# Expert blocks of 32 slots in four column groups in place of 64 slots in two, and GpSimd on two of the last additions

## The chip, the cores and the metric

One NeuronCore of a Trainium2 chip runs the whole program in one launch. The metric is the device time of one execution in microseconds (us). The kernel before took 1650.99 us, the median of 3 runs (1648.49 to 1652.93).

## What is computed

The reference is one layer of a decoder trunk for 256 prompt tokens and 64 sample tokens (320 in all), model width 1024, all in float32. First comes a mixing part (attention, retention, gMLP) and then, with which the change deals, a mixture of 32 experts of which each token uses four:

```python
logits = (x @ router_w) + router_b                 # 320 x 32
top_v, top_i = lax.top_k(logits, 4)
gates = softmax(top_v)
# for every expert e and every token that chose it
hdn = xblk @ w1[e] + b1[e]                         # 1024 -> 2048
g, up = hdn[:, :1024], hdn[:, 1024:]
g, up = minimum(g, 7), clip(up, -7, 7)
act = (up + 1) * (g * sigmoid(1.702 * g))
yb = act @ w2[e] + b2[e]                           # 1024 -> 1024
y[token] += yb * gate
x = x + g2 * y
```

The order of the additions and the size of the expert blocks are the kernel's own affair.

## The kernel before, in words

Five engines run their own programs and meet at semaphores. SyncE (SP) only issues the loads of weights, TensorE (PE) multiplies, ScalarE (ACT) and VectorE (DVE) move results out of PSUM and do the arithmetic on them, GpSimd (POOL) prepares small things and is idle in the expert part.

**Weights.** An expert has 12.6 MB of weights: four units of 2 MB for the hidden layer (units 0 to 3) and two for the layer out (units 4 and 5). They pass through `ring`, which has six slots, one for each unit number, so that the ring holds the weights of exactly one expert. SP walks over the experts; for unit j of the next expert it waits (line 366) until the last block of the expert before has used its own unit j, and then issues the load into that slot (line 367):

```python
with sp.Fori(1, NEXP) as e:
    before = sp.value_load(table_i[0:1, bass.ds(MAX_BLOCKS + 1 + e, 1)], min_val=1, max_val=MAX_BLOCKS)
    for j in range(EXPERT_UNITS):
        sp.wait_ge(unit_used, EXPERT_UNITS * before + j)
        sp.dma_start(ring[:, j, :], ins["w_moe"][bass.ds(e, 1), j, :, :].rearrange("a p n -> p (a n)")).then_inc(unit_in[j], 16)
```

`before` is the number of blocks of all experts ahead of e. PE adds one to `unit_used` each time that a block has used a unit.

**Blocks.** The tokens of an expert are put into blocks of 64 slots. A router stage on DVE counts the tokens of each expert, works out how many blocks each needs (at least one, lines 1097 to 1099), and writes a table of the expert and the first slot of each block. All four engines then loop over the blocks (`Fori(1, n_blocks + 1)`), the blocks of one expert one after another. The 64 slots are the stationary columns of the matmul, so that two matmuls, each on one half of the output columns, stand side by side in the 128 columns of the array: column group a writes partitions 64a to 64a + 63. In one block PE does, in this order:

- hidden: units 0 and 1 into one bank, 2 and 3 into a second (line 1609, 32 matmuls of 512 columns), each pair with two for the bias (line 1614)
- `scatter(i, 0)`: the block before, spread to the first 128 tokens and weighted by the gates (line 1572)
- `gather(i + 1)`: the rows of the next block's tokens, picked out by a 0/1 matrix (line 1558)
- the transposes of the activations, then those of the gates (line 1200), `scatter(i, 1)`
- layer out: unit 4 (line 1638, 8 matmuls), `turn(i + 1)`: the gathered rows of the next block transposed (line 1200), `scatter(i, 2)`, unit 5

The profile shows every float32 matmul twice, as two records; a transpose and the bfloat16 bias matmul are one each. DVE cuts the two hidden halves (lines 1167 and 1169), multiplies them (1173), adds each scattered tile to the sum `U` (1178), and picks the slots of the next block (1143, 1144, 1068, 1159). ACT does the activation (732), and copies the gathered rows (714), the transposed activations (735), the gates (738), the turned rows (718) and the output (741) out of PSUM.

**End.** After the loop DVE multiplies the sum of the three token tiles by the modulation and adds it to the residual (1182, 1184); the last block is scattered by PE into banks of its own (`FINAL_BANKS`), DVE does the same with it (1189, 1192), and SP stores the three tiles.

Of the kernel before, what the change touches and what calls it, by code (L numbers as in the profile page):

```python
# [16 lines left out]
ACT = mybir.ActivationFunctionType  # L17
AX = mybir.AxisListType
# [49 lines left out]
BLOCK = 64  # L68
MAX_BLOCKS = 64
# [58 lines left out]
def build(nc, ctx, ins, outs):  # L128
# [45 lines left out]
    def cut(at, *shape):  # L174
# [52 lines left out]
    of_block = cut(704, 2)  # L227
# [3 lines left out]
    pick_gate = cut(1024, 3, 2, BLOCK)  # L231
    sel_now = cut(1408, 2, 3)
    xgT = cut(1536, 4, 2, BLOCK)
    actT = cut(2048, 4, 2, BLOCK)
    gateT = cut(2560, 3 * P)
    y_blk = cut(2944, HALF)
    g_cut = cut(3456, HALF)
    g_act = cut(3968, HALF)
    u_cut = cut(4480, HALF)
    h_act = cut(4992, HALF)  # L240
    pick_e = cut(5504, BLOCK // 2).bitcast(BF16)

# [10 lines left out]
    xg_s = W[:, 2, 0:HALF]  # L253
# [23 lines left out]
    gate2_ready, gate2_taken, y_clean, sum_clean, qk_normed, max_ready = map(sem, (  # L277
        "gate2_ready", "gate2_taken", "y_clean", "sum_clean", "qk_normed", "max_ready"))
# [8 lines left out]
    turned, b1_in, b1_split, expert_picked = map(sem, (  # L287
        "turned", "b1_in", "b1_split", "expert_picked"))
# [28 lines left out]

    def z_banks(idx):
# [5 lines left out]
    FINAL_BANKS = [6, 0, 2]  # L324
# [57 lines left out]
    def _(pool):  # L382
# [124 lines left out]
        nc.gpsimd.memset(y_blk, 0.0).then_inc(y_clean, 1)  # L507
        pool.wait_ge(y_clean, 1)
        for a in range(2):
            pool.dma_start(y_blk[64 * a:64 * a + NEXP], ins["b2"][:, HALF * a:HALF * a + HALF]).then_inc(b2_in, 16)  # L510
        pool.wait_ge(h_ready, 3)
        nc.gpsimd.memset(U[:, :, :], 0.0).then_inc(sum_clean, 1)


    @block.scalar
    def _(act):
# [195 lines left out]
        def take_gathered(i):  # L712
            act.wait_ge(gathered, i)
            A(xg_s, ps[:, 3, :], ACT.Copy).then_inc(xg_rows, 1)  # L714

        def take_turned(i):
            act.wait_ge(turned, i)
            A(xgT, ps[:, 3, :].rearrange("p (c a s) -> p c a s", c=4, a=2), ACT.Copy).then_inc(xg_ready, 1)
# [8 lines left out]
        act.wait_ge(b2_in, 32)  # L727
        act.sem_inc(y_ready, 1)
        n_blocks = act.value_load(table_i[0:1, MAX_BLOCKS:MAX_BLOCKS + 1], min_val=NEXP, max_val=MAX_BLOCKS - 1)
        with act.Fori(1, n_blocks + 1) as i:  # L730
            act.wait_ge(g_cut_ready, i)
            A(g_act, g_cut, ACT.Gelu_apprx_sigmoid).then_inc(g_act_ready, 1)  # L732
            take_gathered(i + 1)
            act.wait_ge(actT_done, i)
            A(actT, ps[:, 4, :].rearrange("p (c a s) -> p c a s", c=4, a=2), ACT.Copy).then_inc(actT_ready, 1)
            act.wait_ge(gateT_done, i)
            act.wait_ge(scattered, 3 * i)
            A(gateT[:, 0:TOKENS], ps[:, 5, 0:TOKENS], ACT.Copy).then_inc(gateT_ready, 1)  # L738
# [6 lines left out]
    def _(dve):  # L745
# [320 lines left out]
        def pick_slots():  # L1066

            X.tensor_tensor(pick, iota.unsqueeze(1).to_broadcast([P, 3, BLOCK]), sel_now[:, 0, :].unsqueeze(2).to_broadcast([P, 3, BLOCK]), ALU.is_equal).then_inc(picked, 1)  # L1068

# [4 lines left out]
        done(X.memset(gateT, 0.0), added)  # L1074
# [20 lines left out]
        X.tensor_copy(counted, aux_bank("cnt")[:, 0:NEXP]).then_inc(used("cnt"), 1)  # L1095
        aux_taken(dve, "cnt")
        done(X.tensor_scalar(n_of, counted, float(BLOCK), 1.0, ALU.is_gt, ALU.add))
        for m in range(2, TOKENS // BLOCK):
            done(X.scalar_tensor_tensor(out=n_of, in0=counted, scalar=float(BLOCK * m), in1=n_of, op0=ALU.is_gt, op1=ALU.add))
# [36 lines left out]
        done(X.tensor_copy(pick_gate[:, :, :, 0:NEXP], gate_e.unsqueeze(2).to_broadcast([P, 3, 2, NEXP])), gates_ready)  # L1136
# [43 lines left out]
        dve.wait_ge(added, 3 * n_blocks + 1)  # L1180
        for t, r in enumerate(ROWS):
            X.tensor_tensor(U[0:r, t, :], U[0:r, t, :], V[0:r, 2 if t == 2 else 0, :], ALU.mult).then_inc(scaled, 1)
            dve.wait_ge(scaled, t + 1)
            X.tensor_tensor(R[0:r, t, :], R[0:r, t, :], U[0:r, t, :], ALU.add).then_inc(summed, 1)
            dve.wait_ge(summed, t + 1)
        for t, r in enumerate(ROWS):
            dve.wait_ge(scattered, 3 * n_blocks + t + 1)
            first = FINAL_BANKS[t]
            X.tensor_tensor(U[0:r, t, :].rearrange("p (a b) -> p a b", a=2), ps[0:r, first:first + 2, :],
                            V[0:r, 2 if t == 2 else 0, :].rearrange("p (a b) -> p a b", a=2), ALU.mult).then_inc(scaled, 1)  # L1190
            dve.wait_ge(scaled, 3 + t + 1)
# [4 lines left out]
    def _(pe):  # L1196
# [356 lines left out]
        def gather(n):  # L1553

            pe.wait_ge(picked, n)
            for t, r in enumerate(ROWS):
                for a in range(2):
                    last = mm(ps[64 * a:64 * a + 64, 3, :], pick[0:r, t, :], T[0:r, t, HALF * a:HALF * a + HALF],  # L1558
                              start=(t == 0), stop=(t == 2), skip_group_check=True)
            last.then_inc(gathered, 1)  # L1560

        def turn(n):

            pe.wait_ge(xg_rows, n)
            for c in range(4):
                last = tr(ps[:, 3, c * P:(c + 1) * P], xg_s[:, c * P:(c + 1) * P], P)
            last.then_inc(turned, 1)

        def scatter_tile(t, first):

            for a in range(2):
                last = mm(ps[:, first + a, :], gateT[64 * a:64 * a + 64, t * P:(t + 1) * P], y_blk[64 * a:64 * a + 64, :], start=True, stop=True)  # L1572
            last.then_inc(scattered, 1)

        def scatter(n, t):

            pe.wait_ge(added, 3 * n + t - 2)
            scatter_tile(t, 6)

        def filled(j):  # L1580

# [180 lines left out]
```

## Time and profile before

| what | value |
|---|---|
| median of 3 runs | 1650.99 us (1648.49 to 1652.93) |
| the profiled execution, its own time | 1649.28 us |
| its span, first to last instruction | 1647.5 us |
| mean granted TensorE clock | 0.965 of full speed |
| PE busy / its weight loads busy | 1548.8 us (94%) / 661.6 us (40%) |
| DVE / ACT / POOL busy | 474.2 / 318.8 / 108.9 us |
| moved by DMA | 491.95 MB, mean 299 GB/s |

A busy PE is one that has a matmul in flight. The span is what the views of the trace divide; the time of the execution is 1.8 us longer. The expert loop runs from 648.9 us to the end, 60% of the span, and everything that the change touches lies in it, in the few microseconds of routing ahead of it, or behind it.

### The profile page before, as it was taken

The page shows a single profiled execution, that of the slowest core. Times are in us where ns is not written, and L with a number is a line of the kernel's source. Part 1 is how long each engine was busy: PE and PEld are TensorE (multiplying, and loading weights), DVE is VectorE, ACT ScalarE, POOL GpSimd, SP SyncE. Part 2 cuts the span into 40 slices and gives each one's busy share as a digit, 9 for nine tenths or more (in the row PEclk, how much of TensorE's full clock was granted, in tenths as well). Part 3 has the DMA queues.
Part 4 walks back from the last instruction along what each step waited for, and adds up shares of the span by engine and source line. Part 5 has one row for each costly group of instructions (what it writes and reads, how often), then busy time and mean ns, then how long its engine had stood idle before and what let it go on. Part 6 is the DMA issues. An engine that isn't in the chain of part 4 may idle for free.

```text
span 1647.5 us, 20298 instructions
## 1 busy us (share of the span) xinstructions
PE 1548.8 (94%) x8093; PEld 661.6 (40%) x8094; DVE 474.2 (29%) x791; ACT 318.8 (19%) x579; POOL 108.9 (7%) x111
## 2 busy tenths in 40 slices
PE   4989899978989898999999999999999999999996
PEld 4555555545544455333333333333333333333332
DVE  2141222147346254222222222222222222222224
ACT  1123332120231232111111111111111111111110
POOL 0000000120433250000000000000000000000000
PEclk8989998898998997999999999999999999999999
DMA  9462441341332650999999999999593999999993
GB/s 355 185 257 111 194 164 58 115 145 64 128 126 105 240 193 32 415 425 429 428 429 428 428 429 429 428 429 428 239 408 161 415 427 429 429 427 429 429 427 130
DMA packets 38583, 491.95 MB, mean 299 GB/s; under 512 B 4784, under 2 KB 4912, under 8 KB 9744
## 3 DMA queue, kind: packets, MB, share of 16 engines
q1 hardware_dynamic: 34144, 477.33, 70.1%
q0 software_dynamic: 4400, 14.06, 2.8%
q8 instruction: 29, 0.48, 0.1%
q14 instruction: 10, 0.08, 0.0%
HBM read 487.05 MB, written 4.33 MB: 298 GB/s over the span
## 4 chain that ended last, share of the span: by engine, by line
PE 89%; DVE 4%; DMA 3%; ACT 2%; issue 1%; POOL 1%; SPq 0%; DVEq 0%; POOLq 0%; ACTq 0%
PE ps L1609 28%; PE ps L1264 17%; PE ps L1638 15%; PE ps L1572 6%; PE ps L1558 6%; PE ps L1271 4%; PE ps L1200 4%; DMA ring<-in_w_dense 2%; PE ps L1223 1%; PE ps L1216 1%; PE ps L1614 1%; PE ps L1322 1%; PE ps L1342 1%; ACT ring L555 1%; PE ps L1520 1%
## 5 line engine op out<-in xcount | busy, mean ns | idle before, releaser
L1609 PE MATMUL ps<-ring,arena 128*64 128x512 f32 x2176 | 480.2, 594 | 2.9 <-issue 2.9
L1264 PE MATMUL ps<-ring,xT 128*128 128x512 f32 x672 | 306.2, 613 | 3.2 <-DMA ring<-in_w_dense 2.4
L1609 PEld LDWEIGHTS ps<-ring,arena 128*64 128x64 f32 x2176 | 156.7, 137 | 308.2 <-issue 305.6
L1638 PE MATMUL ps<-ring,arena 128*64 128x512 f32 x1088 | 248.5, 598 | 0.0
L1178 DVE TENSOR_TENSOR U<-ps,U 128x1024 f32<-128x1024 f32 (+1 forms) x102 | 124.4, 1220 | 248.9 <-PE ps L1572 248.9
L1264 PEld LDWEIGHTS ps<-ring,xT 128*128 128x128 f32 x672 | 129.2, 196 | 162.6 <-issue 158.2
L1638 PEld LDWEIGHTS ps<-ring,arena 128*64 128x64 f32 x1088 | 72.1, 136 | 168.1 <-issue 142.3
L1572 PE MATMUL ps<-arena 64*128 64x512 f32 x420 | 119.7, 636 | 0.8 <-ACT arena L741 0.8
L1558 PE MATMUL ps<-T,arena 128*64 128x512 f32 (+1 forms) x420 | 104.3, 615 | 1.2 <-DVE arena L1068 1.2
L714 ACT ACTIVATE W<-ps 128x512 f32<-128x512 f32 x35 | 20.9, 598 | 338.5 <-PE ps L1558 338.5
L1169 DVE TENSOR_SCALAR arena<-ps 128x512 f32<-128x512 f32 x34 | 23.5, 692 | 217.5 <-PE ps L1614 217.5
L1271 PE MATMUL ps<-ring,xT 128*64 128x256 f32 x672 | 81.6, 398 | 0.0
L1167 DVE TENSOR_SCALAR arena<-ps 128x512 f32<-128x512 f32 x34 | 23.5, 692 | 187.6 <-PE ps L1614 187.6
L1271 PEld LDWEIGHTS ps<-ring,xT 128*64 128x64 f32 x672 | 48.4, 143 | 33.0 <-issue 12.7
L732 ACT ACTIVATE arena<-arena 128x512 f32<-128x512 f32 x34 | 21.4, 629 | 204.6 <-DVE arena L1167 204.6
L555 ACT ACTIVATE ring<-ps 128x512 f32<-128x512 f32 (+1 forms) x48 | 23.4, 487 | 170.0 <-PE ps L1264 141.4
L1558 PEld LDWEIGHTS ps<-T,arena 128*64 128x64 f32 (+1 forms) x420 | 24.1, 136 | 76.5 <-issue 76.5
L738 ACT ACTIVATE arena<-ps 128x320 f32<-128x320 f32 x34 | 14.9, 437 | 203.5 <-PE ps L1572 203.5
L1200 PEld LDWEIGHTS ps<-consts,arena 128*128 128x128 f32 (+2 forms) x321 | 35.2, 138 | 41.5 <-issue 41.1
L1200 PE MATMUL ps<-consts,arena 128*128 128x128 f32 (+2 forms) x321 | 48.2, 277 | 0.5 <-ACT arena L629 0.5
L1216 PE MATMUL ps<-ring 128*32 128x128 f32 x768 | 29.2, 317 | 18.8 <-DMA ring<-in_w_dense 18.8
L1572 PEld LDWEIGHTS ps<-arena 64*128 64x128 f32 x420 | 33.7, 190 | 29.6 <-issue 29.6
(261 smaller groups left out, 1043.7 us busy)
## 6 DMA issues: line engine op xcount, KB each, us to landing
ring<-in_w_moe SPq DMA_DIRECT2D x192, 2048.0 KB, 14.5
ring<-in_w_dense SPq DMA_DIRECT2D x33, 2048.0 KB, 8.6
V<-in_state POOLq DMA_DIRECT2D x6, 256.0 KB, 8.2
out_sample_retention<-V POOLq DMA_DIRECT2D x6, 256.0 KB, 2.8
R<-in_x_prompt SPq DMA_DIRECT2D x1, 1024.0 KB, 17.1
arena<-in_cache_kT POOLq DMA_DIRECT2D x8, 128.0 KB, 3.5
arena<-in_cache_v POOLq DMA_DIRECT2D x8, 128.0 KB, 3.6
arena<-in_b_gate POOLq DMA_DIRECT2D x4, 256.0 KB, 4.4
```

The lines of the kernel that those rows point to most:

```text
L555: A(buf[0:ROWS[t], t, c0 + c:c0 + c + w], src, func).then_inc(z_used, 1)
L1167: X.tensor_scalar(g_cut, ps[:, 0, :], LIMIT, None, ALU.min).then_inc(g_cut_ready, 1)
L1169: X.tensor_scalar(u_cut, ps[:, 1, :], LIMIT, -LIMIT, ALU.min, ALU.max).then_inc(dve_step, 1)
L1178: X.tensor_tensor(both, ps[0:r, 6:8, :], both, ALU.add).then_inc(added, 1)
L1200: return nc.tensor.transpose(out, in_, ident[0:r, 0:r], **kw)
L1216: last = mm(aux_bank(name)[32 * j:32 * j + 32, 0:128], silu_c[:, k, :], wv[:, k, 128 * j:128 * j + 128], start=(k == 0), stop=(k == KD - 1 ...
L1264: last = mm(banks[t][0], xT[:, k, t * P:t * P + P], wv[:, k, :], start=(k == 0), stop=(k == KD - 1))
L1271: last = mm(banks[2 + a][0], xT[:, k, 2 * P:TOKENS], wv[:, k, 256 * a:256 * a + 256], start=(k == 0), stop=(k == KD - 1), skip_group_check ...
L1558: last = mm(ps[64 * a:64 * a + 64, 3, :], pick[0:r, t, :], T[0:r, t, HALF * a:HALF * a + HALF], start=(t == 0), stop=(t == 2), skip_group_ ...
L1572: last = mm(ps[:, first + a, :], gateT[64 * a:64 * a + 64, t * P:(t + 1) * P], y_blk[64 * a:64 * a + 64, :], start=True, stop=True)
L1609: last = mm(ps[64 * a:64 * a + 64, half, :], xgT[:, k, j % 2, :], wv[:, k, HALF * a:HALF * a + HALF], start=(j % 2 == 0 and k == 0), stop= ...
L1638: last = mm(ps[64 * a:64 * a + 64, 2, :], actT[:, k, j - 4, :], wv[:, k, HALF * a:HALF * a + HALF], start=(j == 4 and k == 0), stop=(j == ...
```

## The change

A block has 32 slots in place of 64, and up to 72 blocks are allowed for. The 32 slots are the stationary columns of a matmul, and four column groups of 32, each on a quarter of the output columns, stand side by side. A unit of the hidden layer now holds two of the eight slices of the contraction, with all 2048 output columns, so that all four hidden units add to one bank; the weights are laid out on the host to fit. Gather, scatter and the layer out work in quarters of 256 columns, and a scatter uses four row groups of 32 slots in place of two of 64. Tiles 0 and 1 of a scatter go together ahead of the gather, tile 2 stays between unit 4 and unit 5; the transposes of the gates move to the end of the block. Ring, slots, SP's loop and its waits are the same. At the end POOL multiplies and adds the sums of tiles 0 and 1 (two operations each), DVE that of tile 2.

```diff
-BLOCK = 64
-MAX_BLOCKS = 64
+BLOCK = 32
+MAX_BLOCKS = 72
+QUARTER = 256
+GROUPS = D // QUARTER
...
+        pool.wait_ge(table_ready, 1)
+        n_blocks = pool.value_load(table_i[0:1, MAX_BLOCKS:MAX_BLOCKS + 1], min_val=NEXP, max_val=MAX_BLOCKS - 1)
+        for t in range(2):
+            pool.wait_ge(added, 3 * n_blocks + t + 1)
+            nc.gpsimd.tensor_tensor(U[:, t, :], U[:, t, :], V[:, 0, :], ALU.mult).then_inc(pool_scaled, 1)
+            pool.wait_ge(pool_scaled, t + 1)
+            nc.gpsimd.tensor_tensor(R[:, t, :], R[:, t, :], U[:, t, :], ALU.add).then_inc(pool_summed, 1)
...
             act.wait_ge(g_cut_ready, i)
             A(g_act, g_cut, ACT.Gelu_apprx_sigmoid).then_inc(g_act_ready, 1)
+            act.wait_ge(actT_done, i)
+            A(actT, ps[:, OUT, 0:QUARTER].rearrange("p (c a s) -> p c a s", c=2, a=GROUPS), ACT.Copy).then_inc(actT_ready, 1)
             take_gathered(i + 1)
...
             take_turned(i + 1)
+            act.wait_ge(scattered, 2 * i)
             act.wait_ge(unit_used, EXPERT_UNITS * i + 5)
-            A(y_blk, ps[:, 2, :], ACT.Copy).then_inc(y_ready, 1)
+            A(y_blk, ps[:, OUT, 0:QUARTER], ACT.Copy).then_inc(y_ready, 1)
+            act.wait_ge(gateT_done, i + 1)
+            A(gateT[:, 0:TOKENS], ps[:, GATES, 0:TOKENS], ACT.Copy).then_inc(gateT_ready, 1)
...
             for t, r in enumerate(ROWS):
-                dve.wait_ge(scattered, 3 * i + t - 2)
-                both = U[0:r, t, :].rearrange("p (a b) -> p a b", a=2)
-                X.tensor_tensor(both, ps[0:r, 6:8, :], both, ALU.add).then_inc(added, 1)
+                dve.wait_ge(scattered, 2 * i - 1 if t < 2 else 2 * i)
+                by_group = U[0:r, t, :].rearrange("p (a c) -> p a c", a=GROUPS)
+                at = QUARTER * (t % 2)
+                X.tensor_tensor(by_group, ps[0:r, SCAT:SCAT + GROUPS, at:at + QUARTER], by_group, ALU.add).then_inc(added, 1)
...
-            for half in range(2):
-                for j in (2 * half, 2 * half + 1):
-                    pe.wait_ge(unit_in[j], 16 * e + 16 * (filled(j) + 1))
-                    wv = ring[:, j, :].rearrange("p (k c) -> p k c", k=4)
-                    for k in range(4):
-                        for a in range(2):
-                            last = mm(ps[64 * a:64 * a + 64, half, :], xgT[:, k, j % 2, :], wv[:, k, HALF * a:HALF * a + HALF],
-                                      start=(j % 2 == 0 and k == 0), stop=False, skip_group_check=True)
...
+            for j in range(4):
+                pe.wait_ge(unit_in[j], 16 * e + 16 * (filled(j) + 1))
+                wv = ring[:, j, :].rearrange("p (k a c) -> p k a c", k=2, a=GROUPS)
+                for k in range(2):
+                    c, b = divmod(2 * j + k, GROUPS)
+                    for a in range(GROUPS):
+                        last = mm(ps[32 * a:32 * a + 32, HID, :], xgT[:, c, b, :], wv[:, k, a, :],
+                                  start=(j == 0 and k == 0), stop=False, skip_group_check=True)
...
             pe.wait_ge(y_ready, i)
             pe.wait_ge(gateT_ready, i)
-            scatter(i, 0)
-            gather(i + 1)
+            scatter_prompt(3 * i)
+            pe.wait_ge(picked, i + 1)
+            gather(0)
+            gather(1)
             pe.wait_ge(act_ready, i)
-            for c in range(4):
-                last = tr(ps[:, 4, c * P:(c + 1) * P], h_act[:, c * P:(c + 1) * P], P)
+            for c in range(2):
+                last = tr(ps[:, OUT, c * P:(c + 1) * P], h_act[:, c * P:(c + 1) * P], P)
             last.then_inc(actT_done, 1)
...
-            scatter(i, 1)
+            gather(2).then_inc(gathered, 1)
...
                 if j == 4:
                     turn(i + 1)
-                    scatter(i, 2)
+                    pe.wait_ge(added, 3 * i + 2)
+                    scatter_tile(2, SCAT, 0).then_inc(scattered, 1)
+            pe.wait_ge(gates_picked, i)
+            for t, r in enumerate(ROWS):
+                last = tr(ps[:, GATES, t * P:t * P + r], pick_gate[0:r, t, :, :], r)
+            last.then_inc(gateT_done, 1)
```

PE, from the wait for unit 5 to the first unit of the next block. In these rows `x7` counts matmuls (not records) of one kind, sizes are output rows x columns, and the semaphores are those that the first one waits for; `ring` holds the weights, `arena` the small operands. Before, the end of the loop and its beginning:

```order
L1638 MATMUL ps<-ring,arena 64x512 [waits unit_in5]
L1638 MATMUL ps<-ring,arena 64x512 x7
L1598 ISA
L1598 COMPARE_AND_BRANCH
...
L1605 ISA [waits expert_picked,xg_ready]
L1609 MATMUL ps<-ring,arena 64x512 [waits unit_in0]
L1609 MATMUL ps<-ring,arena 64x512 x7
L1609 MATMUL ps<-ring,arena 64x512 [waits unit_in1]
```

and now:

```order
L1656 MATMUL ps<-ring,arena 32x256 [waits unit_in5]
L1656 MATMUL ps<-ring,arena 32x256 x15
L1219 MATMUL ps<-consts,arena 128x128 [waits gates_picked]
L1219 MATMUL ps<-consts,arena 128x128
L1219 MATMUL ps<-consts,arena 128x64
L1618 ISA
L1618 COMPARE_AND_BRANCH
...
L1624 ISA [waits expert_picked,xg_ready]
L1629 MATMUL ps<-ring,arena 32x512 [waits unit_in0]
L1629 MATMUL ps<-ring,arena 32x512 x7
```

Between unit 5 of a block and unit 0 of the next stand now the three transposes of the gates, and a unit out is 16 matmuls of 256 columns where it was 8 of 512.

PE, between the last hidden matmul and unit 4, now (before, there were one scatter tile, six gather matmuls, four transposes of the activations, three of the gates and a second scatter tile at this place):

```order
L1634 MATMUL ps<-consts,arena 32x512 x4
L1596 REGISTER_ALU [waits gateT_ready,y_ready]
L1591 MATMUL ps<-arena 128x256 [waits added]
L1591 MATMUL ps<-arena 128x256 x7
L1641 REGISTER_ALU
L1576 MATMUL ps<-T,arena 32x256 [waits picked]
L1576 MATMUL ps<-T,arena 32x256 x7
L1219 MATMUL ps<-consts,arena 128x128 [waits act_ready]
L1219 MATMUL ps<-consts,arena 128x128
L1576 MATMUL ps<-T,arena 32x256 x4
L1656 MATMUL ps<-ring,arena 32x256 [waits unit_in4,actT_ready]
```

The third tile of the gather now stands between the transposes of the activations and unit 4, and both scatters of prompt tokens stand ahead of the gather.

## Rows read from the trace of the kernel before

**Rows 1.** Page: span; busy time, share and instructions of each engine.
```profile
span 1647.5 us, 20298 instructions
PE 1548.8 (94%) x8093; PEld 661.6 (40%) x8094; DVE 474.2 (29%) x791; ACT 318.8 (19%) x579; POOL 108.9 (7%) x111
```
**Rows 2.** Lines 1167 and 1609: count, ns min/median/max, first and last start in us, shape.
```profile
L1167 DVE TENSOR_SCALAR arena<-ps x34: 691/692/692, 657.9 to 1609.9; 128x512 f32<-128x512 f32 x34
...
L1609 PE MATMUL ps<-ring,arena x2176: 590/592/1061, 648.9 to 1616.1; 128*64 128x512 f32 x198
```
**Rows 3.** Stretches: us, busy PE, PEld, DVE, ACT, POOL (count), granted clock, DMA share, GB/s.
```profile
700.00:1140.00 440.00, 440.00 (x2061) 147.29 (x2059) 105.75 (x167) 70.04 (x107) 0.00 (x0) 1.00 1.01 428
...
1156.00:1173.66 17.66, 17.66 (x83) 5.96 (x83) 5.62 (x10) 3.98 (x6) 0.00 (x0) 1.00 0.07 28
1173.66:1181.30 7.64, 7.64 (x40) 2.60 (x38) 0.69 (x1) 0.63 (x1) 0.00 (x0) 1.00 0.88 332
```
**Rows 4.** Expert weights: issues, KB each, median us to landing; then line 367's min/median/max.
```profile
ring<-in_w_moe SPq DMA_DIRECT2D x192, 2048.0 KB, 14.5
...
DMA to landing us min/median/max: 7.5/14.5/23.0
```
**Rows 5.** Timeline of PE, one block: start, us, line, records.
```profile
1148.11 7.04 PE L1609 MATMUL ps<-ring,arena 128*64 128x512 f32 x32
1154.98 0.39 PE L1614 MATMUL ps<-consts,arena 96*64 96x512 bf16 x2
1155.30 1.13 PE L1572 MATMUL ps<-arena 64*128 64x512 f32 x4
1156.36 2.94 PE L1558 MATMUL ps<-T,arena 128*64 128x512 f32 x12
1159.23 1.08 PE L1200 MATMUL ps<-consts,arena 128*128 128x128 f32 x7
1160.05 1.18 PE L1572 MATMUL ps<-arena 64*128 64x512 f32 x4
1161.16 3.65 PE L1638 MATMUL ps<-ring,arena 128*64 128x512 f32 x16
...
1166.39 3.65 PE L1638 MATMUL ps<-ring,arena 128*64 128x512 f32 x16
1169.87 7.04 PE L1609 MATMUL ps<-ring,arena 128*64 128x512 f32 x32
```
**Rows 6.** Timeline of PE, the first matmuls with four column groups of 32.
```profile
19.27 3.64 PE L1216 MATMUL ps<-ring 128*32 128x128 f32 x64 [4.36 <-DMA ring<-in_w_dense]
...
36.37 1.96 PE L1216 MATMUL ps<-ring 128*32 128x128 f32 x64 [2.95 <-DMA ring<-in_w_dense]
```
**Rows 7.** Stretches, as rows 3: those two, and the start of the expert loop.
```profile
19.20:22.90 3.70, 3.63 (x64) 2.96 (x64) 0.00 (x0) 0.00 (x0) 0.00 (x0) 0.50 1.03 269
...
36.30:38.30 2.00, 1.93 (x64) 1.69 (x64) 0.19 (x1) 0.00 (x0) 0.87 (x2) 1.00 0.96 399
...
648.80:654.40 5.60, 5.51 (x18) 1.82 (x20) 0.00 (x0) 0.08 (x1) 0.00 (x0) 0.70 0.01 3
```
**Rows 8.** Timeline, start of the expert loop.
```profile
648.89 8.78 PE L1609 MATMUL ps<-ring,arena 128*64 128x512 f32 x32 [2.90 <-issue]
654.42 11.06 SPq L367 DMA_DIRECT2D ring<-in_w_moe  x4
```
**Rows 9.** Groups by line (page): busy us, mean ns of one, idle before, releaser.
```profile
L1178 DVE TENSOR_TENSOR U<-ps,U 128x1024 f32<-128x1024 f32 (+1 forms) x102 | 124.4, 1220 | 248.9 <-PE ps L1572 248.9
...
L738 ACT ACTIVATE arena<-ps 128x320 f32<-128x320 f32 x34 | 14.9, 437 | 203.5 <-PE ps L1572 203.5
```
**Rows 10.** The end: timeline of DVE and SP; one line of POOL.
```profile
1642.89 1.22 DVE L1192 TENSOR_TENSOR R<-R,U 64x1024 f32<-64x1024 f32 x1
1644.13 0.53 SPq L372 DMA_DIRECT2D out_y_sample<-R  x1
...
L476 POOL TENSOR_TENSOR ring<-ring x3: 2333/2337/3322, 518.5 to 523.1; 128x1024 f32<-128x1024 f32 x2, 64x1024 f32<-64x1024 f32 x1
```

More of the change, by code:

```diff
@@ L1094, in _ @@
         counted = rtmp[:, 1, :]
[L1095 removed]
+        X.tensor_scalar(counted, aux_bank("cnt")[:, 0:NEXP], 1.0 / BLOCK, None, ALU.mult).then_inc(used("cnt"), 1)
         aux_taken(dve, "cnt")
[L1097 to L1099 removed]
+        limits = TOKENS // BLOCK - 1
+        done(X.tensor_tensor(over, counted.unsqueeze(2).to_broadcast([P, NEXP, limits]),
+                             iota[:, 1:1 + limits].unsqueeze(1).to_broadcast([P, NEXP, limits]), ALU.is_gt))
+        done(X.tensor_reduce(n_of, over, AX.X, ALU.add))
+        done(X.tensor_scalar(n_of, n_of, 1.0, None, ALU.add))
         done(X.tensor_tensor_scan(out=cum_of, data0=ones[:, 0:NEXP], data1=n_of, initial=0.0, op0=ALU.mult, op1=ALU.add))
@@ L1551, in _, with gather, scatter_tile, scatter_prompt @@
            start=True, stop=True).then_inc(aux_ready, 1)
[L1553 to L1560, printed above, removed]
+        def gather(t):
+            r = ROWS[t]
+            for a in range(GROUPS):
+                last = mm(ps[32 * a:32 * a + 32, ROWSB, 0:QUARTER], pick[0:r, t, :], T[0:r, t, QUARTER * a:QUARTER * a + QUARTER],
+                          start=(t == 0), stop=(t == 2), skip_group_check=True)
+            return last
         def turn(n):
             pe.wait_ge(xg_rows, n)
-            for c in range(4):
-                last = tr(ps[:, 3, c * P:(c + 1) * P], xg_s[:, c * P:(c + 1) * P], P)
+            for c in range(2):
+                last = tr(ps[:, ROWSB, c * P:(c + 1) * P], xg_s[:, c * P:(c + 1) * P], P)
             last.then_inc(turned, 1)
[L1569 to L1580, printed above, removed]
-            return DENSE_UNITS // DENSE_SLOTS if j < DENSE_SLOTS else 0
+        def scatter_tile(t, first, at):
+            r = ROWS[t]
+            for a in range(GROUPS):
+                last = mm(ps[0:r, first + a, at:at + QUARTER], gateT[32 * a:32 * a + 32, t * P:t * P + r], y_blk[32 * a:32 * a + 32, :], start=True, stop=True)
+            return last
+        def scatter_prompt(waited):
+            pe.wait_ge(added, waited)
+            scatter_tile(0, SCAT, 0)
+            scatter_tile(1, SCAT, QUARTER).then_inc(scattered, 1)
         pe.wait_ge(gate2_taken, 4)
-        gather(1)
+        pe.wait_ge(picked, 1)
+        for t in range(3):
+            last = gather(t)
+        last.then_inc(gathered, 1)
         turn(1)
@@ L1595, in _ @@
         pe.wait_ge(b1_split, 12)
+        pe.sem_inc(gateT_done, 1)
         pe.sem_inc(unit_used, EXPERT_UNITS - 1)
@@ L1618, in _ @@
+            for a in range(GROUPS):
+                last = mm(ps[32 * a:32 * a + 32, HID, :], pick_e[0:96], b1_by_group[0:96, :, a, :],
+                          start=False, stop=True, skip_group_check=True)
+            last.then_inc(unit_used, 1)
             pe.wait_ge(y_ready, i)
             pe.wait_ge(gateT_ready, i)
-            scatter(i, 0)
-            gather(i + 1)
+            scatter_prompt(3 * i)
+            pe.wait_ge(picked, i + 1)
+            gather(0)
+            gather(1)
@@ L1634, in _ @@
                 pe.wait_ge(unit_in[j], 16 * e + 16 * (filled(j) + 1))
-                wv = ring[:, j, :].rearrange("p (k c) -> p k c", k=4)
-                for k in range(4):
-                    for a in range(2):
-                        last = mm(ps[64 * a:64 * a + 64, 2, :], actT[:, k, j - 4, :], wv[:, k, HALF * a:HALF * a + HALF],
-                                  start=(j == 4 and k == 0), stop=(j == 5 and k == 3), skip_group_check=True)
+                wv = ring[:, j, :].rearrange("p (k c) -> p k c", k=GROUPS)
+                for b in range(GROUPS):
+                    for a in range(GROUPS):
+                        last = mm(ps[32 * a:32 * a + 32, OUT, 0:QUARTER], actT[:, j - 4, b, :], wv[:, b, QUARTER * a:QUARTER * a + QUARTER],
+                                  start=(j == 4 and b == 0), stop=(j == 5 and b == 3), skip_group_check=True)
                 last.then_inc(unit_used, 1)
```

118 lines of the change are left out of this document (54 added, 64 removed).

## The prediction

> **What bounds the kernel now.** I read the page first, then the expert loop block by block, then the loads. The page shows PE busy for 94% of the span [rows 1]. Line 1167 runs once per block: 34 times, its starts 952.0 us apart from first to last [rows 2], so that a block takes 952.0 / 33 = 28.85 us, and all blocks the same. In the stretch from 700 to 1140 us PE is busy throughout at the full clock, and so is DMA, at 428 GB/s [rows 3]. The two nearly tie: six units of 2048 KB are 12.58 MB, 29.4 us of loads per expert against 28.85 us of PE. Who waits for whom shows where an expert has two blocks: PE works on without a gap, while DMA falls to 28 GB/s for 17.66 us [rows 3], since the ring holds one expert and a slot comes free only in the expert's last block. So PE sets the pace, and DMA has almost nothing to spare: 31 experts x 6 units x 4.89 us (2.097 MB at 429 GB/s) = 909.5 us of pure loading lie within a loop of 998.6.
>
> **How many blocks.** Counting the choices of the reference's router on its inputs, 8 experts have at most 32 tokens, 22 have 33 to 64, and two have 66. With 64 slots that gives 30 + 2 x 2 = 34 blocks, as the trace has it [rows 2]; with 32 slots 8 + 44 + 6 = 58. The last expert and the first have one block each.
>
> **The change on PE.** A record of 512 columns takes 6.87 / 32 = 0.215 us in the stream of pairs [rows 5], with two side by side. Four column groups are to be seen in line 1216: 64 records of 128 columns in 1.96 us, 31 ns each with the run-out of the last [rows 6]; one by itself would take 2 x 0.215 x 128 / 512 = 0.107 us, so 3.5 of four at least ran at once, and without the run-out all four. I take 0.107 us per record of 512 and 0.054 per record of 256. A new unit is 16 records of 512 or 32 of 256: 1.72 us either way, where it was 3.44. A transpose is 0.107 us, and turning from one kind of matmul to another costs 0.1 to 0.3 us (12 gather records from 1156.36 to 1159.23: 2.87 us for 2.58 of work [rows 5]); I take 0.2. One block is then four hidden units 6.88, bias 0.42, two scatter tiles 1.06, two gather tiles 1.06, two transposes 0.41, gather 0.63, unit 4 1.92, turn 0.41, scatter 0.63, unit 5 1.92, gates 0.52: **15.9 us**. 58 such blocks are 922 us where 34 x 28.85 were 981. The page "TensorE: Matmul & The Clock Gate" of the Trainium skill (Part 3, "Measured speedup vs the span model") gives three column groups as 2.38 times one; by that ratio hidden and unit out would be a quarter longer, and the sum below some 30 us higher; the trace's 1.96 us speaks against it.
>
> No row has four row groups (the scatter). Two at once have a row: 4 records of 512 in 1.06 us [rows 5]. A tile costs 0.43 us if all four run at once, 0.86 in pairs; I take 0.43, and the other adds 0.9 us ahead of unit 4, where, below, 1.5 us are free.
>
> **The change on the loads.** This is the term that decides. Loads, slots and waits are the same; when a slot comes free is not. In a two-block expert the first block needs all six units and frees none. Once unit 5 has landed, nothing is left to load until the second block has used unit 0. Behind that landing PE does unit 5 (1.92), the transposes of the gates (0.52), which stand there now, and unit 0 of the second block (1.72 and the run-out of its last record, 0.592 - 0.215 = 0.38 [rows 2]): 4.5 us. Then the load starts from nothing: the fastest landing of a unit is 7.5 us [rows 4] for 4.89 of transfer, so 2.6 us are lost to the start. The trace has such a restart: unit 0 of a second block is done at 1169.87 + 3.44 + 0.38 = 1173.69 [rows 5], and from there the rate comes back [rows 3]. **Each of the 24 experts with two or three blocks thus stops the loads for 4.5 + 2.6 = 7.1 us**, a three-block one for another whole block, 15.9. Such an expert takes 29.4 + 7.1 = 36.5 us, for two blocks of 15.9: PE waits, and the loads with their stops set the pace. One-block experts run at 29.4.
>
> Before, these stops hit two experts and cost nothing beyond PE's own 28.85; now they hit 24.
>
> **The sum, on the span.**
> - First slot free: was 654.4, after 16 records from 648.89 on, much of them at half clock [rows 7, 8]. At half clock 16 new ones take 3.4 and the run-out 0.4: 652.7.
> - Loading 186 units: 909.5.
> - 25 starts from nothing (the first and 24) x 2.6: 65.
> - 24 x 4.5 us of PE between last landing and first free slot: 108.
> - Two whole middle blocks: 31.8.
> - Behind the last landing: unit 5 2.1, the copies of output and gates by ACT (0.44 for 320 columns [rows 9]) 1.1, scatter 1.3, six DVE operations of 1.22 and a gap = 7.5, and the store, 3.4 from the last DVE operation to the end of the span [rows 1, 10]: 15.4.
>
> Together 1782.4. POOL's four operations take 2.33 us each [rows 10] and start with the last block's first addition, some 5 us ahead of the last landing; they end ahead of DVE's turn and cost nothing, and if they did not, some 3 us.
>
> DVE has three additions of 1.22 per block [rows 9], in all about 7 us of work in a block of 16 to 18; ACT has less. Both lie under PE's work and waits, at no cost; uncovered, an addition held up would push the scatter behind unit 4, where 1.5 us are free (PE is through with that scatter 8.3 us after unit 3 landed, unit 5 lands after 9.8). The routing ahead of the loop has a compare and a reduction over 288 numbers in place of three small operations, under half a us.
>
> **The clock.** PE now waits up to 4.9 - 1.7 = 3.2 us for units 2 and 3. A wait of 2.95 us left the granted clock at 1.00 (64 records in 1.96 us, 2.4 GHz), one of 4.36 us did not (3.64 us, 0.50, 1.2 GHz) [rows 6, 7]. Bounds: nothing, or 4.3 us of work from unit 3 to unit 4 at half clock in each of the 24, less the 1.5 free: 2.8 x 24 = 67. Being nearer to 2.95, I take a third, 22.
>
> 1782.4 + 22.3 = 1804.7 for the span. The profiled execution took 1649.28 for a span of 1647.5; with the same 1.8 the forecast is **1806 us**, 157 over that execution (the median of the runs shown is 1.7 higher still).
>
> **Rivals.**
> - *The clock is lost in every such expert* and is still low in the stop: 67 in place of 22, and 3.8 us of unit 5, transposes and unit 0 twice as long, x 24 = 91: 1782.4 + 158 + 1.8 = **1942**. For it: 4.36 us was enough, and short bursts may not bring the clock back: it was 0.50 in the burst behind that wait [rows 7]. Against: PE works almost without a gap from unit 3 to unit 5. The Trainium skill's "TensorE: Matmul & The Clock Gate" ("HAM oscillation") describes this very case, a matmul that waits for each slice of its weights and runs each at the lower clock; by it this rival would be the likeliest, and the 2.95 us row disagrees.
> - *The other side: the loads do not stop.* If a slot came free before the last unit of its expert had landed, only loading would remain: 652.7 + 2.6 + 909.5 + 15.4 + 1.8 = **1582**. The point that decides is the stop's length: below (1649 - 1582) / 24 = 2.8 us the change would gain. For it: PE's work does shrink from 981 to 922 us. Against: the start alone costs 2.6, and the one stop shown lasted as long as PE needed [rows 3].
> - *The groups don't run four at a time* but two, so that the change doesn't do what it says: hidden 13.8, out 6.9, the rest as before, about 28 us x 58 = 1640, from 648.9 on: **2310**. Against: line 1216 [rows 6].
>
> **Chances.** Forecast 0.73 (its own range 1770 to 1850), clock rival, whole or half, 0.18, loads without a stop 0.04, pairs 0.03, anything else 0.02. The low end of the range is the sum without the clock term and with turns of 0.1 us, 1770; the high end takes in about half of the clock rival, 1880. A measurement here tells 0.3%, 5 us, from no change: slower 0.95, same 0.01, faster 0.04.
>
> **What would show it.** In the profile after: 58 records where line 1167 had 34; hidden units of 1.7 us with waits for DMA ahead of them; PE busy well below 90% of the loop; in each two-block expert a stretch of about 5 us with DMA near 0 GB/s between the last landing and the next issue; a period near 36.5 us for such experts and 29.4 for the others; a few granted clocks of 0.50. Wrong would be a loop without such gaps, a period of 32 us or less for two-block experts, or hidden units of 3.4 us at the full clock.

## The result and the profile after

The changed kernel takes **1790.97 us** (median of 3 runs, 1786.05 to 1797.63), 1.085 times the kernel before [95% interval 1.081 to 1.090]. The forecast was 1806, with a range of 1770 to 1880. The profiled execution took 1797.63 us for a span of 1795.8, the longest of the three.

The page of the changed kernel: span; busy time, share and instructions; the chain that ended last by engine; and the costliest group (busy us, mean ns | idle before it, and what ended that).

```profile
span 1795.8 us, 34114 instructions
PE 1535.4 (86%) x14371; PEld 697.0 (39%) x14372; DVE 578.6 (32%) x1050; ACT 374.7 (21%) x747; POOL 121.0 (7%) x116
...
PE 55%; DMA 38%; DVE 3%; ACT 2%; issue 1%; POOL 1%; SPq 0%; DVEq 0%; POOLq 0%; ACTq 0%
...
L1629 PE MATMUL ps<-ring,arena 128*32 128x512 f32 x3712 | 468.8, 647 | 143.9 <-DMA ring<-in_w_moe 140.9
```

PE is busy 13 us less than before [rows 1], but the span is 148 us longer. Ahead of the hidden matmuls (line 1629, line 1609 before) it now waits 141 us for loads, and 38% of the last chain is DMA. The once-per-block instruction, the first cut on DVE, shows that the blocks are as many as counted, where [rows 2] had 34:

```profile
L1185 DVE TENSOR_SCALAR arena<-ps x58: 424/424/426, 658.8 to 1772.5; 128x256 f32<-128x256 f32 x58
```

Here is PE's timeline from the first block of a two-block expert to its second (start, us, line, records, wait in brackets).

```profile
1128.81 1.92 PE L1629 MATMUL ps<-ring,arena 128*32 128x512 f32 x16 [0.49 <-DMA ring<-in_w_moe]
1133.70 2.77 PE L1629 MATMUL ps<-ring,arena 128*32 128x512 f32 x16 [2.97 <-DMA ring<-in_w_moe]
...
1140.42 1.93 PE L1656 MATMUL ps<-ring,arena 128*32 128x256 f32 x32
1142.28 0.44 PE L1219 MATMUL ps<-consts,arena 128*128 128x128 f32 x2
1142.65 0.66 PE L1591 MATMUL ps<-arena 32*64 32x256 f32 x8
1143.48 1.93 PE L1656 MATMUL ps<-ring,arena 128*32 128x256 f32 x32 [0.17 <-DMA ring<-in_w_moe]
1145.35 0.64 PE L1219 MATMUL ps<-consts,arena 128*128 128x128 f32 x3
1145.92 7.07 PE L1629 MATMUL ps<-ring,arena 128*32 128x512 f32 x64
1152.81 0.40 PE L1634 MATMUL ps<-consts,arena 96*32 96x512 bf16 x4
1153.14 1.15 PE L1591 MATMUL ps<-arena 32*128 32x256 f32 x16
1154.22 1.07 PE L1576 MATMUL ps<-T,arena 128*32 128x256 f32 x16
```

Unit 5 lands at 1143.44. From there PE does unit 5, the three transposes of the gates, and, from 1145.92, unit 0 of the second block. SP issues the next load at 1148.05, 4.6 us after the landing. The table of stretches (us, busy PE, PEld, DVE, ACT, POOL, granted clock, DMA share, GB/s) shows that nothing moves in that time, and what follows:

```profile
1143.45:1147.95 4.50, 4.47 (x55) 1.95 (x59) 2.26 (x5) 2.10 (x3) 0.00 (x0) 1.00 0.00 0
1147.95:1155.62 7.67, 7.67 (x90) 2.79 (x84) 2.23 (x5) 0.42 (x1) 0.00 (x0) 1.00 0.89 333
1155.62:1180.10 24.48, 19.33 (x238) 7.46 (x237) 8.39 (x14) 4.82 (x10) 0.00 (x0) 1.00 0.96 410
```

The stretches of 0 and of 333 GB/s are the stop and the start from nothing; in [rows 3], before, the loads ran at 428 GB/s and stopped only in the two experts with two blocks. From the landing times of unit 5, one expert to the next: 29.37 us in the six experts with one block, 36.6 to 36.9 in nineteen with two, 37.1 to 37.9 in three more of them, 52.2 and 52.4 in the two with three blocks.

### The profile page after: what moved, and what is told of

Read it like the earlier page. It is cut to its first block, busy times and chain, and to the rows that moved or that the text cites. A ratio compares the mean times of both kernels' runs of the same rounds, so it can differ in the third digit from the quotient of the medians.

```text
span 1795.8 us, 34114 instructions
## 1 busy us (share of the span) xinstructions
PE 1535.4 (86%) x14371; PEld 697.0 (39%) x14372; DVE 578.6 (32%) x1050; ACT 374.7 (21%) x747; POOL 121.0 (7%) x116
## 4 chain that ended last, share of the span: by engine, by line
PE 55%; DMA 38%; DVE 3%; ACT 2%; issue 1%; POOL 1%; SPq 0%; DVEq 0%; POOLq 0%; ACTq 0%
DMA ring<-in_w_moe 35%; PE ps L1283 15%; PE ps L1629 12%; PE ps L1656 8%; PE ps L1290 4%; PE ps L1219 3%; PE ps L1591 3%; PE ps L1576 3%; DMA ring<-in_w_dense 2%; PE ps L1242 1%; PE ps L1235 1%; PE ps L1341 1%; PE ps L1361 1%; ACT ring L570 1%; PE ps L1539 0%
## 5 line engine op out<-in xcount | busy, mean ns | idle before, releaser
L1629 PE MATMUL ps<-ring,arena 128*32 128x512 f32 x3712 | 468.8, 647 | 143.9 <-DMA ring<-in_w_moe 140.9
L1629 PEld LDWEIGHTS ps<-ring,arena 128*32 128x32 f32 x3712 | 112.0, 114 | 436.9 <-issue 221.0
L1196 DVE TENSOR_TENSOR U<-ps,U 128x1024 f32<-128x1024 f32 x174 | 206.9, 1217 | 132.7 <-PE ps L1591 132.6
L1656 PE MATMUL ps<-ring,arena 128*32 128x256 f32 x3712 | 224.3, 382 | 21.9 <-DMA ring<-in_w_moe 21.6
L1656 PEld LDWEIGHTS ps<-ring,arena 128*32 128x32 f32 x3712 | 108.7, 109 | 129.8 <-DMA ring<-in_w_moe 35.0
L1591 PE MATMUL ps<-arena 32*128 32x256 f32 (+1 forms) x1416 | 113.1, 421 | 0.7 <-issue 0.7
L1576 PE MATMUL ps<-T,arena 128*32 128x256 f32 (+1 forms) x1416 | 101.9, 390 | 0.8 <-DVE arena L1083 0.8
L1219 PE MATMUL ps<-consts,arena 128*128 128x128 f32 (+2 forms) x491 | 100.2, 292 | 1.0 <-ACT arena L729 0.5
L1591 PEld LDWEIGHTS ps<-arena 32*128 32x128 f32 (+1 forms) x1416 | 59.2, 180 | 60.6 <-issue 58.1
L747 ACT ACT_TABLE_LOAD x58 | 74.4, 1283 | 2.1 <-issue 1.1
L1177 DVE TENSOR_TENSOR arena<-arena 128x384 f32<-128x384 f32 x58 | 32.4, 558 | 97.7 <-PE ps L1219 95.8
L1576 PEld LDWEIGHTS ps<-T,arena 128*32 128x32 f32 (+1 forms) x1416 | 34.0, 108 | 42.2 <-issue 32.2
```

Source lines behind the costliest of these rows:

```text
L1196: X.tensor_tensor(by_group, ps[0:r, SCAT:SCAT + GROUPS, at:at + QUARTER], by_group, ALU.add).then_inc(added, 1)
L1219: return nc.tensor.transpose(out, in_, ident[0:r, 0:r], **kw)
L1576: last = mm(ps[32 * a:32 * a + 32, ROWSB, 0:QUARTER], pick[0:r, t, :], T[0:r, t, QUARTER * a:QUARTER * a + QUARTER], start=(t == 0), stop= ...
L1591: last = mm(ps[0:r, first + a, at:at + QUARTER], gateT[32 * a:32 * a + 32, t * P:t * P + r], y_blk[32 * a:32 * a + 32, :], start=True, sto ...
L1629: last = mm(ps[32 * a:32 * a + 32, HID, :], xgT[:, c, b, :], wv[:, k, a, :], start=(j == 0 and k == 0), stop=False, skip_group_check=True)
L1656: last = mm(ps[32 * a:32 * a + 32, OUT, 0:QUARTER], actT[:, j - 4, b, :], wv[:, b, QUARTER * a:QUARTER * a + QUARTER], start=(j == 4 and b ...
```

## Experiments

Beside the median stands the **loading time** of the profiled execution, because the part ahead of the expert loop ended some 10 us sooner or later from one execution to the next. It runs from the landing of the last unit of the first expert that SP's loop loads to the last landing of all. It is 1092.04 us in the changed kernel (686.62 to 1778.66) and 927.76 in the one before. It can differ by 2.6 us between two executions of the same loop: experiment 5, which leaves the loop as it is, has 1089.48. The kernel before was run beside all of them: 1649.6 us (11 runs) and 1648.2 (17 runs).

The theory is that of the prediction: loads with their stops set the pace. The rivals are a price per block, wherever it lies, and the lost clock.

### 1. One block for every expert

```diff
-        done(X.tensor_scalar(n_of, n_of, 1.0, None, ALU.add))
+        done(X.tensor_scalar(n_of, n_of, 0.0, 1.0, ALU.mult, ALU.add))
```

> The changed kernel with one block per expert: tokens beyond an expert's first 32 are left out, so 32 blocks in place of 58, and no expert has a second block. Stopped loads (each of 24 experts holds all six slots until its second block uses unit 0): only pure loading is left, 686.6 us (landing of the first loaded expert) + 30 x 29.37 + 17.1 behind the last landing + 1.8 = 1587 us, DMA at 428 GB/s without a gap. Price per block (the 58 blocks themselves, at (1791 - 649) / 58 = 19.7 us each, are what became longer): 32 blocks would be worth 630 us, and the loads a floor of 910, so also about 1587; but then DMA would already lie near its ceiling in the changed kernel. Lost clock: PE waits most of the time here and the clock falls most often, so if the clock set the pace this would stay above 1650.

Measured: 1584.36 us (2 runs), 0.960 of the kernel before [0.956, 0.965]. Every expert takes 29.33 to 29.38 us. In the long stretch the loads never stop (columns as above), though the granted clock is at 0.86:

```profile
700.00:1560.00 860.00, 570.52 (x5451) 183.97 (x5443) 170.65 (x319) 106.64 (x203) 0.00 (x0) 0.86 1.01 428
```

So without second blocks only loading remains, and PE's half clock, 265 us of the expert loop in this execution, costs nothing where PE waits anyway.

### 2. The gates' transposes out of the stop

```diff
                     scatter_tile(2, SCAT, 0).then_inc(scattered, 1)
-            pe.wait_ge(gates_picked, i)
-            for t, r in enumerate(ROWS):
-                last = tr(ps[:, GATES, t * P:t * P + r], pick_gate[0:r, t, :, :], r)
-            last.then_inc(gateT_done, 1)
+                    pe.wait_ge(gates_picked, i)
+                    for t, r in enumerate(ROWS):
+                        last = tr(ps[:, GATES, t * P:t * P + r], pick_gate[0:r, t, :, :], r)
+                    last.then_inc(gateT_done, 1)
```

They now stand between units 4 and 5, ahead of the last landing.

> The three transposes of the gates moved from behind unit 5 to ahead of the wait for unit 5. PE does the same work in all. Stopped loads: 0.5 us less between last landing and first free slot, in each of 24 experts, so 12 us less (1791 to 1779), and 36.25 us in place of 36.75 per two-block expert. PE's total work or the clock: no change within 5 us.

Measured: 1781.6 us (6 runs), 1.080 of before [1.077, 1.084], 9.4 less than the change as it is; the loading time is 1079.62, 12.4 less. PE's timeline around a stop, from the landing of unit 5 at 1134.18 to the next issue at 1138.54:

```profile
1134.05 0.64 PE L1219 MATMUL ps<-consts,arena 128*128 128x128 f32 x3
1134.62 1.93 PE L1656 MATMUL ps<-ring,arena 128*32 128x256 f32 x32
1136.42 7.07 PE L1629 MATMUL ps<-ring,arena 128*32 128x512 f32 x64
```

The same work, moved by one place, gains because it leaves the stop. That is no price per block: the work is still done 58 times. The gain splits: where unit 5 was not late the stop fell from 4.61 to 3.97 us, the full length of the transposes; where the clock had been low before it, as here, only to some 4.3, since the transposes use up the slack ahead of unit 5 and delay it. That makes 9 of the 12.4 us; 2 more are three late starts of unit 5 in the changed kernel's execution (below), which not every execution has.

### 3. The gates' transposes five times

```diff
-            for t, r in enumerate(ROWS):
-                last = tr(ps[:, GATES, t * P:t * P + r], pick_gate[0:r, t, :, :], r)
+            for _ in range(5):
+                for t, r in enumerate(ROWS):
+                    last = tr(ps[:, GATES, t * P:t * P + r], pick_gate[0:r, t, :, :], r)
```

> The three transposes of the gates done five times behind unit 5, 12 more of them, some 1.3 us per block at the full clock. Stopped loads: 24 stops longer by 1.3 and the two three-block experts' middle blocks too: 26 x 1.3 = 34 us more (1825). Price per block: 58 x 1.3 = 75 us more (1866). One-block experts keep 29.4 us by the first and lengthen by the second.

Measured: 1862.56 us (4 runs), 1.128 of before [1.123, 1.132]: 72 more, by the number alone the rival's result. The form is the theory's: one-block experts still take 29.36 us, two-block ones 38.9 to 39.2 or 40.5 to 40.8. PE's timeline at two of the stops:

```profile
1043.00 3.39 PE L1656 MATMUL ps<-ring,arena 128*32 128x256 f32 x32 [1.81 <-DMA ring<-in_w_moe]
1046.32 3.12 PE L1219 MATMUL ps<-consts,arena 128*128 128x128 f32 x15
1049.37 7.07 PE L1629 MATMUL ps<-ring,arena 128*32 128x512 f32 x64
...
1062.42 1.93 PE L1656 MATMUL ps<-ring,arena 128*32 128x256 f32 x32
1064.28 2.93 PE L1219 MATMUL ps<-consts,arena 128*128 128x128 f32 x15
1067.14 3.21 PE L1629 MATMUL ps<-ring,arena 128*32 128x512 f32 x28
```

The first stop is a first block's, with the clock low in unit 5 (3.32 us from start to start); the second stretch is a second block, at full clock. Fifteen transposes take 2.86 us (1064.28 to 1067.14), 0.19 each, so that 2.29 were added and not the 1.3 that I had expected with 0.107 each. And in 12 of the 24 stops the clock was low, 1.6 us more. 24 x 2.29 + 12 x 1.6 + 2 middle blocks x 2.28 = 79, less the 2 that late starts of unit 5 cost in the changed kernel (below): 77. The loading time grew by 76.1. The theory stands, my price of a transpose fell.

### 4. PE kept busy ahead of unit 3

```diff
             for j in range(4):
+                if j == 3:
+                    pe.wait_ge(added, 3 * i)
+                    for _ in range(8):
+                        mm(ps[0:32, SCAT, 0:128], ident[:, 0:32], ident, start=True, stop=True)
                 pe.wait_ge(unit_in[j], 16 * e + 16 * (filled(j) + 1))
```

The spare matmuls fill part of the 2.97 us wait and write where nobody reads.

> Before the wait for unit 3 PE does eight small matmuls into a bank that the scatter overwrites later (16 records, 1.7 us), so that it does not sit idle there; nothing is left out. It measures what the lost clock costs in the changed kernel. Clock worth little (it is lost in gaps whose delay the next wait absorbs): the granted clock rises above 0.94 and the time stays at 1791 within 5 us (the two three-block experts' middle blocks add 3.4, a few us come back). Clock worth the 22 us of the prediction or more: 1770 or less.

Measured: 1809.49 us (6 runs), 1.097 of before [1.093, 1.101]: 18.5 more, which neither side had. The clock now held through unit 3 in every such expert. But in 9 of 24 it was lost one wait later, ahead of unit 5, as PE's timeline shows for two experts next to each other:

```profile
1035.42 1.93 PE L1660 MATMUL ps<-ring,arena 128*32 128x256 f32 x32 [1.80 <-DMA ring<-in_w_moe]
1037.29 0.64 PE L1219 MATMUL ps<-consts,arena 128*128 128x128 f32 x3
1037.86 5.36 PE L1633 MATMUL ps<-ring,arena 128*32 128x512 f32 x48
...
1062.26 1.92 PE L1633 MATMUL ps<-ring,arena 128*32 128x512 f32 x16
...
1072.05 3.62 PE L1660 MATMUL ps<-ring,arena 128*32 128x256 f32 x32 [1.81 <-DMA ring<-in_w_moe]
1075.60 0.64 PE L1219 MATMUL ps<-consts,arena 128*128 128x128 f32 x3
1076.17 4.07 PE L1633 MATMUL ps<-ring,arena 128*32 128x512 f32 x36
```

Unit 3 of the second, at 1062.26, runs at the full clock. The same wait ahead of unit 5, and that unit takes 1.87 us in one expert and 3.55 in the other. There the loss lies in the stop, which is 4.61 us in fifteen experts and 6.1 to 6.3 in the nine. 9 x 1.6, and 1.72 of spare matmuls in each of the two middle blocks, less the 2: 15.8, and the loading time grew by 15.8. So a lost clock costs where it falls into the stop, and next to nothing ahead of it.

### 5. The end without GpSimd

```diff
-            nc.gpsimd.tensor_tensor(U[:, t, :], U[:, t, :], V[:, 0, :], ALU.mult).then_inc(pool_scaled, 1)
...
+            X.tensor_tensor(U[:, t, :], U[:, t, :], V[:, 0, :], ALU.mult).then_inc(pool_scaled, 1)
```

and so with the addition behind it: DVE does both for tiles 0 and 1.

> The changed kernel without GpSimd's part: DVE does the multiplications and additions of tiles 0 and 1 itself behind the loop. Read on the stretch from the last landing of a weight unit to the end of the span, 17.1 us in the changed kernel. If sharing with GpSimd helps: DVE has four more operations of 1.25 us behind its last addition, the stretch grows to about 20 us. If it does not, because GpSimd and DVE slow each other down there (DVE's addition on tile 2 took 3.25 us beside GpSimd, where it takes 1.22 alone): 17 us or less. Either way under 0.2% of the time.

Measured, in one run: 1793.79 us. The last landing is at 1772.7, the end of the span at 1792.0: 19.3 us, against 17.1 with GpSimd (1778.66 to 1795.8). The sharing is worth 2.1 us, in one execution of each (with the clock lost in the last expert in both), not the 4 x 1.23 that DVE no longer does. Why, the timelines of the end show: DVE, then POOL, of the changed kernel, and DVE's same two operations in this experiment.

```profile
1779.86 1.22 DVE L1199 TENSOR_TENSOR U<-U,V 64x1024 f32<-64x1024 f32 x1
1781.11 3.25 DVE L1201 TENSOR_TENSOR R<-R,U 64x1024 f32<-64x1024 f32 x1
1784.57 1.23 DVE L1208 TENSOR_TENSOR U<-ps,V 128x1024 f32<-128x1024 f32 x1 [0.20 <-DVE R L1201]
1785.83 1.83 DVE L1211 TENSOR_TENSOR R<-R,U 128x1024 f32<-128x1024 f32 x1
```

```profile
1775.17 2.37 POOL L525 TENSOR_TENSOR U<-U,V 128x1024 f32<-128x1024 f32 x1 [1147.10 <-DVE U L1196]
1777.62 2.37 POOL L527 TENSOR_TENSOR R<-R,U 128x1024 f32<-128x1024 f32 x1
1779.95 3.34 POOL L525 TENSOR_TENSOR U<-U,V 128x1024 f32<-128x1024 f32 x1
1783.37 3.21 POOL L527 TENSOR_TENSOR R<-R,U 128x1024 f32<-128x1024 f32 x1
```

```profile
1778.70 1.21 DVE L1196 TENSOR_TENSOR U<-U,V 64x1024 f32<-64x1024 f32 x1
1779.94 1.22 DVE L1198 TENSOR_TENSOR R<-R,U 64x1024 f32<-64x1024 f32 x1
```

The addition to `R` takes DVE 3.25 us beside POOL and 1.22 without it.

### 6. The next block's units 0 and 1 ahead of the layer out

The slots of units 0 and 1 now come free before units 4 and 5 are even used; units 4 and 5 count in a semaphore of their own, and the gather and turn of the next block move up.

```diff
-                sp.wait_ge(unit_used, EXPERT_UNITS * before + j)
+                if j < 4:
+                    sp.wait_ge(unit_used, 4 * before + j)
+                else:
+                    sp.wait_ge(out_used, 2 * before + (j - 4))
...
+            turn(i + 1)
+            e_next = pe.value_load(table_i[0:1, bass.ds(i, 1)], min_val=0, max_val=NEXP - 1)
+            pe.wait_ge(xg_ready, i + 1)
+            hidden(0, e_next)
+            hidden(1, e_next)
 
             pe.wait_ge(actT_ready, i)
```

> Hidden units 0 and 1 of the next block moved ahead of the layer out of the current one (turn and third gather tile moved ahead with them), so that a second block frees slots 0 and 1 before units 4 and 5 of its expert have landed; SP waits for units 0 to 3 and for 4 and 5 on two counters. PE's work is the same. Stopped loads: the stop of 7 us disappears in 22 two-block experts and shrinks to about 14 us in the two three-block ones; the pace becomes PE's 31 us in runs of two-block experts and DMA's 29.4 elsewhere: 1640 to 1670 us. Price per block or clock: no change, 1780 to 1800.

Measured: 1682.86 us (4 runs), 1.019 of before [1.014, 1.024]; the loading time is 982.39, 110 less. A two-block expert takes 30.9 to 31.2 us behind a one-block expert, and 32.3 to 32.9 in a row of such experts. The stops shrink to 0.6 us at most, save 16.9 and 16.6 in the two experts with three blocks, and with them go three quarters of the loss (108 of 141 us, by the medians). The time missed the expected 1640 to 1670, because PE becomes the bound. Its timeline in one block of 16.3 us (970.60 to 986.92):

```profile
969.04 1.01 PE L1222 MATMUL ps<-consts,arena 128*128 128x128 f32 x4
970.60 3.64 PE L1630 MATMUL ps<-ring,arena 128*32 128x512 f32 x32 [0.55 <-ACT arena L736]
974.05 1.92 PE L1671 MATMUL ps<-ring,arena 128*32 128x256 f32 x32
...
986.92 3.64 PE L1630 MATMUL ps<-ring,arena 128*32 128x512 f32 x32 [0.55 <-ACT arena L736]
```

PE waits 0.55 us for ACT's copy of the turned rows, which the new order put on its path.

### 7. As 6, with the gates' transposes in that gap and the third scatter tile behind unit 5

Against experiment 6:

```diff
             turn(i + 1)
+            pe.wait_ge(gates_picked, i)
+            for t, r in enumerate(ROWS):
+                last = tr(ps[:, GATES, t * P:t * P + r], pick_gate[0:r, t, :, :], r)
+            last.then_inc(gateT_done, 1)
             e_next = pe.value_load(table_i[0:1, bass.ds(i, 1)], min_val=0, max_val=NEXP - 1)
...
-                if j == 4:
-                    pe.wait_ge(added, 3 * i + 2)
-                    scatter_tile(2, SCAT, 0).then_inc(scattered, 1)
...
+            pe.wait_ge(added, 3 * i + 2)
+            scatter_tile(2, SCAT, 0).then_inc(scattered, 1)
```

> As the run with the next block's hidden units 0 and 1 ahead of the layer out, with like matmuls put together: the gates' transposes stand beside the turn, where PE waited 0.55 us per block, and the third scatter tile behind unit 5. With the stops gone PE's own block sets the pace in runs of two-block experts (16.3 us there). If that is the bound now: two changes of the array's division fewer and the wait filled, about 15.5 us per block, 31 per two-block expert, and 1683 falls to 1645 to 1655, even with the kernel before. If something else is (a remaining stop of the loads): no change from 1683.

Measured: 1656.11 us (12 runs), 1.006 of before [1.003, 1.009]. PE's timeline of one whole block, 959.99 to 975.60:

```profile
959.99 3.64 PE L1630 MATMUL ps<-ring,arena 128*32 128x512 f32 x32
...
966.43 1.43 PE L1222 MATMUL ps<-consts,arena 128*128 128x128 f32 x7
967.99 3.64 PE L1630 MATMUL ps<-ring,arena 128*32 128x512 f32 x32
971.44 3.64 PE L1675 MATMUL ps<-ring,arena 128*32 128x256 f32 x64
975.01 0.66 PE L1594 MATMUL ps<-arena 32*64 32x256 f32 x8
975.60 3.64 PE L1630 MATMUL ps<-ring,arena 128*32 128x512 f32 x32
```

A block of 15.6 us makes a two-block expert 31.2, above the 29.4 of loading and the 28.85 of one 64-slot block [rows 2]. This is the best order of 32-slot blocks that I found. It ends 0.6% behind the kernel before; no version here that computes every token beats that one.

## Why the prediction was right, point by point

- **First slot free**: forecast 652.7, measured 653.45.
- **PE's work**: right in kind. Sixteen hidden records take 1.72 us, four column groups run at once, and so do the scatter's four row groups, which no row before had shown: 16 records of 256 columns in 1.08 us (1153.14 to 1154.22), in fours that start within 0.02 us, the fours 0.22 us apart once they run. Line 1283, without groups, needs 0.43 us per record of 512, so that each four took the time of one. The Trainium skill's "TensorE: Matmul & The Clock Gate" (Part 3, "Measured speedup vs the span model") gives four row groups as 3.07 times one. The trace doesn't agree: those fours ran as four. A middle block took 15.5 us where the sum had 15.9; a transpose alone was mispriced (0.19 us, not 0.107 and a turn).
- **The stop**: forecast 4.5 us, measured 4.61 in 21 of the 24. Experiments 1, 2 and 6 show that it is the cause: without second blocks no stop and no loss, half a us of work out of it shortens it by up to its length, and slots freed early take 110 of the loss away.
- **The start from nothing**: forecast 2.6 us, measured 36.75 - 29.36 - 4.61 = 2.8. That and the stop's 0.1, over the 24 experts, are 7 of the sum's miss.
- **The clock**: the term that failed, 22 us forecast ("I take a third") and 2.2 measured in the loop. The clock was lost more often than that: PE needs 3.15 us from the start of unit 3 to the gather at full clock, 4.5 to 4.8 in fourteen of the 24 experts and 5.3 to 6.0 in three. The Trainium skill's "TensorE: Matmul & The Clock Gate" ("HAM oscillation") has this mechanism, and by it the clock rival would have been the likeliest; the trace agrees that the clock falls, not that it costs. What was mis-sized was the price, 2.8 us each. Most losses are 1.4 to 1.7 us, and the slack ahead of unit 5 is 1.8 (the wait of experiment 4), not 1.5. Only three overran it, by 1.0, 1.0 and 0.3, and how many do varies from run to run: in experiment 5, with the same loop, the clock was lost in 13 of the 24, none overran, and all stops are 4.61, but for the two that a middle block lengthens. One of the three, with unit 5 starting at 753.78 for a landing at 752.78:

```profile
743.03 3.64 PE L1629 MATMUL ps<-ring,arena 128*32 128x512 f32 x16 [1.76 <-DMA ring<-in_w_moe]
...
749.02 1.07 PE L1576 MATMUL ps<-T,arena 128*32 128x256 f32 x16
...
753.78 1.93 PE L1656 MATMUL ps<-ring,arena 128*32 128x256 f32 x32
```

- **The end**: forecast 15.4 us, measured 17.1. The step was "they end ahead of DVE's turn and cost nothing, and if they did not, some 3 us": POOL ended at 1786.58, between DVE's last operations, and DVE lost 2.0 us in one addition and 0.6 in another. The step alone is not the whole 1.7: in experiments 1 and 4 the additions took the same 3.27 and 1.83 us, and the end 15.7. There the clock held in the last expert, and DVE came to tile 2 some 1.7 us ahead of the last landing; in the changed kernel's execution it was lost (unit 3 to the gather 4.8 us), DVE came only with the landing, and the held-up addition was in the way of the last block. So 1.4 of the 1.7 needed the lost clock too.
- **The sum** without the clock term was 1782.4 for a span of 1795.8: 0.8 from the first slot, 1.2 from the first loaded expert (33.2 us, 31.9 forecast), 9.5 from the two-block experts (the 7, and 2.2 of the clock), 1.7 from the end. With 22 for the clock it came out 9 above that span, and the forecast 15 above the median. That it is so near is in part luck: an excess in one term covered small deficits in four.

The rival on the other side, loads without a stop, gave 1582 as the time; experiment 1, which makes its condition true by leaving out all tokens past an expert's first 32, took 1584.

## What to carry to other kernels

When a buffer holds exactly one set of operands, look for the place where the last load has landed and the first slot is not yet free: everything between these two points is paid in full, once per set that is used twice, and making the work elsewhere faster doesn't touch it. An instruction's price depends on whether it lies in that stretch: half a us of transposes moved out of it was worth some 10 us in all, and a clock loss of 1.6 us cost all of it inside that stretch and, with few exceptions, nothing ahead of it. Free the first slots early, by doing the next pass's first pieces before this pass's last, and then check which engine is the next bound.

## What the hardware showed that I had not expected

- **POOL and DVE block each other when both read two operands from SBUF.** DVE's addition began at 1781.11 and ended at 1784.36, 1.07 us after POOL's operation ended (1783.29); POOL's next one, from 1783.37, took 3.21 us in place of 2.37, so about as long as if it had begun when DVE ended. DVE's multiplication with one operand in PSUM (1784.57) took its 1.23 us beside the same POOL operation. Experiments 1 to 4 show the same again (DVE's addition 3.25 to 3.27, POOL's two 3.33 or 3.34 and 3.21); in experiment 7, where POOL was through before DVE began, POOL took 2.35 to 2.38 and DVE 1.22. The Trainium skill's "SBUF — State Buffer" ("Who interferes with whom") says so: a DVE instruction with two SBUF inputs contends with a GpSimd one that reads SBUF, and the port pair that they share is locked by one of them at a time. The rows agree.
- **The length of a wait didn't tell whether the clock was lost.** Behind waits of 2.97 us unit 3 ran at full clock in seven experts and slower in others; behind 1.80 and 1.81 us unit 5 ran at full and at half clock (experiment 4). What decides it these runs leave open.
